# A one-core hybrid encoder block: dot products of the last 16 tokens before or after the start of the second expert pass

## The reference

```
idx = jnp.take_along_axis(cidx.reshape(TB, PH, K * K), pos, axis=-1)
g = jax.nn.softmax(top_s, axis=-1).astype(xb.dtype)
u = expert_u[idx]
a = jax.nn.gelu(jnp.einsum('td,thkd->thk', xb, u), approximate=False)
return jnp.einsum('thk,thkd->td', g * a, expert_v[idx])
```

## Time and profile before

| | us |
|---|---|
| three runs | 950.32, 951.26, 952.13 |
| median | 951.26 |
| the profiled execution's own time | 951.26 |
| its span, first to last instruction | 949.5 |

### The profile page before, as it was taken

The page is one execution under the profiler, slowest core; times in us unless marked ns, Lnnn a source line. Parts: engine busy times, 40 slices in busy tenths (PEclk is TensorE's granted clock), DMA queues, the critical chain, the costliest instruction groups (busy, mean ns, idle before and its releaser), DMA issues.

```text
span 949.5 us, 21518 instructions
## 1 busy us (share of the span) xinstructions
PE 942.1 (99%) x7332; PEld 905.1 (95%) x7332; DVE 780.5 (82%) x1622; ACT 557.4 (59%) x994; POOL 347.4 (37%) x202
## 2 busy tenths in 40 slices
PE   9999999999999999999999999999999999999997
PEld 9999899999999999999999999999999999999997
DVE  7988878889799997777787774788888888888776
ACT  6556764666665646666766765555555555555545
POOL 0000000067878787888888876111000100000000
PEclk9999999999999999999999999999999999999999
DMA  8887667666579998999999999999999999998981
GB/s 304 262 242 206 198 202 237 211 206 203 181 223 261 244 237 224 261 268 274 231 268 265 239 229 248 313 366 321 319 317 332 332 332 322 317 322 273 294 259 45
DMA packets 134332, 246.63 MB, mean 260 GB/s; under 512 B 32032, under 2 KB 81056, under 8 KB 134000
## 3 DMA queue, kind: packets, MB, share of 16 engines
q1 hardware_dynamic: 110656, 227.73, 74.8%
q0 software_dynamic: 23168, 17.12, 9.9%
q10 hardware_dynamic: 432, 0.80, 0.2%
HBM read 219.21 MB, written 26.35 MB: 259 GB/s over the span
## 4 chain that ended last, share of the span: by engine, by line
PE 94%; DVE 3%; issue 1%; ACT 1%; DMA 1%; DVEq 0%; ACTq 0%
PE pOO L1462 45%; PE pOO L1741 8%; PE pTT L1758 6%; PE pOO L1758 6%; PE pMM L1758 6%; PE pSS L1758 6%; PE pMM L1759 3%; PE pOO L1759 3%; PE pTT L1759 3%; PE pSS L1759 3%; DVE wlos L918 1%; PE pSS L1527 1%; PE pSS L1683 1%; PE pSS L1716 1%; PE pTT L1716 1%
## 5 line engine op out<-in xcount | busy, mean ns | idle before, releaser
L653 ACT ACTIVATE whis<-raw 128x1024 fp32r<-128x1024 f32 x326 | 344.2, 1057 | 172.6 <-PE pSS L1759 140.6
L1462 PE MATMUL pOO<-xhi,whis 128*128 128x240 f32 (+1 forms) x1040 | 288.1, 277 | 0.0
L1462 PE MATMUL pOO<-xlo,whis 128*128 128x240 f32 (+1 forms) x1040 | 286.1, 275 | 0.0
L1462 PE MATMUL pOO<-xhi,wlos 128*128 128x240 f32 (+1 forms) x1040 | 286.1, 275 | 0.0
L628 POOL DMA_INDIRECT g_scratch<-small x128 | 234.1, 1829 | 51.0 <-issue 37.0
L918 DVE TENSOR_TENSOR wlos<-raw,whis 128x1024 fp32r<-128x1024 f32 x172 | 209.1, 1219 | 42.7 <-ACT whis L653 42.1
L1462 PEld LDWEIGHTS pOO<-xhi,whis 128*128 128x128 f32 x1040 | 196.3, 189 | 1.4 <-issue 1.3
L1462 PEld LDWEIGHTS pOO<-xlo,whis 128*128 128x128 f32 x1040 | 196.3, 189 | 0.0
L1462 PEld LDWEIGHTS pOO<-xhi,wlos 128*128 128x128 f32 x1040 | 196.3, 189 | 0.0
L1343 DVE TENSOR_TENSOR wlos<-raw,whis 128x1024 fp32r<-128x1024 f32 x125 | 153.0, 1224 | 49.6 <-ACT whis L653 48.0
L596 POOL TENSOR_TENSOR wlos<-raw,whis 128x1024 fp32r<-128x1024 f32 x30 | 72.2, 2416 | 213.6 <-ACT whis L653 213.3
(11 more groups left out here) (297 smaller groups left out, 1976.5 us busy)
## 6 DMA issues: line engine op xcount, KB each, us to landing
raw<-in_stream SPq DMA_DIRECT2D x199, 512.0 KB, 4.4
raw<-in_vrows SPq DMA_DIRECT2D x128, 512.0 KB, 4.9
a_scratch<-ast SPq DMA_DIRECT2D x128, 120.0 KB, 3.1
held<-a_scratch SPq DMA_DIRECT2D x128, 120.0 KB, 4.5
g_scratch<-ghot SPq DMA_DIRECT2D x32, 256.0 KB, 4.5
held<-g_scratch SPq DMA_DIRECT2D x124, 64.0 KB, 4.3
biasm<-in_bias SPq DMA_DIRECT2D x8, 256.0 KB, 5.4
g_scratch<-small POOLq DMA_INDIRECT x128
```

The lines of the kernel that those rows point to most:

```text
L653: act.activation(whi[s], raw[s][:], ACT.Copy).then_inc(hi_ready, 1)
L1462: last = pe.matmul(dst, st, mv, start=(c == 0 and q == 0), stop=(c == len(terms) - 1 and q == 2))
```

## The change

The number of dot rounds in the U pass rises from 8 to 14. Their gathers go in threes ahead of scatter heads 3 to 6, and two ahead of head 7, which had none. Two dot rounds are left in the V pass, at other places. The first row of `expert_v` is gathered at V tile 2 in place of 31, the last at 99 in place of 91; rows are added behind groups 5 to 27 in place of 10 to 25. Apart from this the first two `low` products of the V pass move, on DVE, from ahead of the `wlos` of V tile 1 to behind it.

```diff
-DOTS_U = 8
-DOT_TILES_U = (65, 73, 76, 84, 89, 97, 105, 113)
-GATHERS_U = {3: (0, 1), 4: (2, 3), 5: (4, 5), 6: (6, 7)}
+DOTS_U = 14
+DOT_TILES_U = (65, 68, 73, 76, 81, 84, 89, 92, 97, 105, 108, 113, 119, 124)
+GATHERS_U = {3: (0, 1, 2), 4: (3, 4, 5), 5: (6, 7, 8), 6: (9, 10, 11), 7: (12, 13)}
...
-DOT_TILES = (2, 5, 8, 11, 15, 19, 23, 27)
-DOT_GROUPS = (2, 3, 4, 5, 6, 7, 8, 9)
-GELU_GROUPS = (2, 12)
-SHARE_GROUPS = (3, 13)
-ROW_TILES = tuple(31 + 4 * m for m in range(TOPK))
-ROW_GROUPS = tuple(10 + m for m in range(TOPK))
+DOT_TILES = (10, 20)
+DOT_GROUPS = (4, 7)
+GELU_GROUPS = (2, 9)
+SHARE_GROUPS = (3, 11)
+ROW_TILES = (2, 9, 16, 23, 33, 39, 45, 51, 57, 63, 69, 75, 81, 87, 93, 99)
+ROW_GROUPS = (5, 6, 8, 9, 10, 12, 13, 15, 16, 18, 19, 21, 22, 24, 25, 27)
...
-                if i == NE_TILES - 1:
-                    low(0, 0)
-                    low(1, 1)
                 low_w(T_U + i + LO_LEAD)
...
+            low(0, 0)
+            low(1, 1)
             low_w(T_V + LEAD - 1)
```

## The result

The changed kernel takes 958.75 us in the median of seven runs (953.05 to 960.94), against 951.26 for the kernel before. The ratio is 1.006, with a 95% interval of 1.0033 to 1.0089. So it is slower by 0.6%, where I had forecast no change and a time of 951.2 within 949.9 to 953.0. With the runs that belong to the profiles, eleven executions are known: 950.86, 953.05, 955.4, 957.6, 957.98, 958.41, 958.58, 958.75, 958.8, 958.91, 960.94. The profiled one is that of 957.98, with a span of 956.2. This scatter of 10 us is itself a finding, since the kernel before stayed within 4.5 us in 77 executions beside the experiments (949.47 to 953.99).

The account below looks back on a forecast made before the run. PE was taken to bound both passes. The seam gave -0.03 us and dots, gathers and rows of V cost 0, so 951.26 - 0.03 = 951.2 us, within 949.9 to 953.0.

Parts of the forecast that it names:

- The spare time: Table load before V tile 0: second piece lands 6.0 us before its reading, so POOL's delay costs PE 0.
- The delay: Six more gathers on POOL delay the scatters by 2.9 us, taken as one step, 2.7; far ends 5.4 and 7.9.
- the two gathers of head 7: On POOL ahead of head 7: they cost nothing, within a wait of 3.21 us; 1.4 at the high gather price.
- A dot doesn't hold POOL: U pass, DVE beside POOL: only a wlos holds a scatter back, read from the scatter of 457.73.
- Rival (3): Scatters end too late, six dots each holding one for 1.2 us: 3.3 us on PE, 954.5; chance 0.04.
- the two old stops: PE stops at V tiles 2 and 4 in the kernel before, 0.66 us together, forecast to swallow the seam's new stop.
- The seam: Between U and V pass: V tile 0 runs 0.63 us late, stops at tiles 2 and 4 vanish, net -0.03.
- The dots in the U pass: On DVE: six more dots at about 1.30 us each, 7.8 us moved from the V pass, cost 0.
- Rival (2): U pass: three gathers in a row crowd out tile loads, PE stops, 2 to 4 us, 954; chance 0.08.
- The rows of V: End of V pass: last add done at 898.1, PE takes the sum at 918.20, 20 us left, cost 0.

Follow-up runs that it names:

- experiment 5: The kernel before, unchanged, profiled a second time: 951.32 us.
- experiment 1: The kernel before with only the two low products of the seam moved behind the wlos of V tile 1: 951.09 us, ratio 1.0.
- experiment 4: The kernel before with six more DVE operations of a dot's kind and size in the U pass, results unused: 950.89 us, ratio 0.9995.
- experiment 12: The kernel before with the whis of V tile 2 ahead of the gelu of the last U tile: 951.96 us, ratio 1.0006.
- experiment 3: The kernel before with six more gathers at the changed kernel's places, into free buffers nobody reads: 956.58 us, ratio 1.0052.
- experiment 7: The changed kernel with 52 PE products on old data ahead of V tile 0: 957.35 us, ratio 1.0068.
- experiment 8: The kernel before with ten dots in the U pass, the two further gathers ahead of head 7: 951.22 us, ratio 1.0001.
- experiment 9: The changed kernel without the last four scatters of head 7: 950.9 us, ratio 0.9998.
- experiment 6: The kernel before with 5.03 us of memsets on POOL ahead of head 7, no DMA added: 955.95 us, ratio 1.0044.
- experiment 10: The changed kernel with one wlos less on POOL ahead of its first scatter, given to DVE: 952.89 us, ratio 1.0042.
- experiment 11: The kernel before with twelve dots in the U pass, third gathers at heads 3 to 6, none at head 7: 951.24 us, ratio 1.0013.
- experiment 2: The changed kernel with the two low products put back ahead of the wlos of V tile 1: 956.81 us, ratio 1.0039.

## Why the prediction was wrong

**The spare time (the step that failed first).** The prediction took 6.0 us between the landing of the table's second piece (load at 589.26, landed about 594.3) and its reading at 600.28. The arithmetic was right and the row was real, but it came from the earliest of five executions with that many gathers. In the others the load comes at 595.95 to 597.02, and the same sum (5.0 to land) leaves -0.7 to -1.7 us. In experiment 5 `weights` waits 1.94 us already; in 1, 4 and 12 it doesn't wait, as a piece can land in 2.4 us. A first sign stood in the groups: the earlier trace rows gives waits of 0.30 and 0.57 at heads 6 and 5 against 1.57 and 3.21 at heads 3 and 7, so the chain's length hung on how each wait fell. I used one execution for a margin that the next could lose.

**The delay (under-sized).** Forecast 2.9 us, taken as one step of a tile, 2.7, with 5.4 and 7.9 as ends. Against the usual chain of before it is one step in experiments 3 and 7 and two, 5.4 us, in the changed kernel; against the first profile it is five, 13.4. Seen against the second profile of before it is 4.4 at the table load and 5.2 at the last scatter; against the first one 12.1 and 12.9. The sum had gathers and waits, and put at nothing that the scatters themselves get slower; of the five steps they are 7.7 us. A gather was set at 1.26 with its issue. Those of the changed kernel take 1.34 + 0.30 in the mean, and at head 4 the second and third took 1.98 and 1.86. Heads 3 to 6 took 559.08 - 404.91 = 154.17 us to the next head's start, against 554.92 - 403.76 = 151.16 in the second profile of before. The forecast of nothing for the two gathers of head 7 was right in experiment 8, where 0.79 us of the wait were left; in the changed kernel they leave none. A later head 7 has more of its scatters in the last tiles, at 2.67 us each: ten, against eight in the second profile of before (571.65 to 590.32) and five in the first.

**"A dot doesn't hold POOL" (misread).** The row it was read from, the scatter of 457.73, had begun 0.72 us ahead of its dot. Where the dot begins first it holds the scatter to 1.42 us behind its own end, as a `wlos` does (495.20, experiment 4). The Trainium skill (SBUF — State Buffer, section on the two separate sides) says that a VectorE operation with two SBUF inputs and a GpSimd operation that reads SBUF exclude each other: whichever starts first has the port pair that they share for its whole length. The trace agrees for a dot or `wlos` that starts first. The other way round it doesn't show the rule, as a dot that starts behind a scatter takes its usual 1.22 to 1.27 us.

**The price of the stop (left out).** Rival (3) took PE's wait as the whole cost. With the wait comes a restart at half clock, 2.3 us after a stop of 5.6. The profiled execution lies 3.5 us over the rival's 954.5: a wait of 5.6 in place of 3.3 and the half clock, less the two old stops and a front shorter by 0.5.

**Rival (3) itself** named the right place, the scatters that end too late, with a chance of 0.04. Its mechanism, every one of six dots holding a scatter for 1.2 us, is not what happened: six more dots alone leave the chain at 305.63 us against 305.62, with a ratio of 0.9995 (experiment 4). Six more gathers alone make the loss (experiment 3). A held scatter can add to it: those of 495.20 and 498.07 are where the changed kernel falls behind experiment 7. The chance should have been built on the end of the scatters, by whatever cause, and not on that one cause.

**Right were** these steps. The seam: forecast 0.63 late at V tile 0 and no stop at tiles 2 and 4, seen so in experiment 9. The dots in the U pass at no cost on DVE, with PE at 155.00 of 155.00 us. Rival (2), crowding, doesn't happen: PE doesn't stop in the U pass. The rows of V in time: the last add is at 903.55, done at 904.83, and PE takes the sum at 924.91, 20 us later, as forecast. Beyond the restart at its start no time came from the V pass.

**Open.** That a few hundredths or tenths of a us decide whether a scatter or DVE's instruction goes first, and that the chain then differs by whole tiles, is in the rows. What moves those starts from one execution to the next isn't settled. Head 1 took 34.96 us in the first profile of before and 34.51 in experiment 6, in all other profiles 37.0 or more. Experiments 6, 10 and 11 show two groups of times, and I have profiles of the lower group only. Why a piece of the table lands in 2.5 us in one execution and in 5.4 in another isn't known either.

## What to carry to other kernels

A margin that ends a chain of a hundred small waits is a spread, not a number: before a change leans on it, look at a second profile, or at the same margin in any other profile of nearly the same kernel. Gathers hide in a queue's wait only as long as that wait lasts; the one that doesn't fit costs its full issue time, and everything behind it in the queue shares the bill. Where the end of such a chain meets a saturated PE, price the step, which is the wait and the restart at half clock together.

## What the runs showed of the hardware

- PE's clock and the stop before it: after stops of 0.40 to 1.22 us (experiments 1, 5, 9, 12) nothing changed; after 3.19 us (experiment 3) the clock fell about 0.7 us after the restart and was 0.50 for some 3.4 us; in stops of 4.44 and 5.59 us (experiment 2, the changed kernel) it had fallen before PE went on, and was 0.50 from the first product on, for about 6 and 4.4 us. With products on old data through the wait it stayed at 1.00. From V tile 0 to the products of the sum it took 317.03, 318.23 and 317.49 us in these three, and 315.20 at full clock: 1.8 to 3.0 us.
- POOL's scatters and DVE: the one that begins first goes on, and a scatter that begins under a running `wlos` or dot (1.22 us each) ends 1.4 us or more behind it. The same scatter took 1.55 us when it began 0.01 us ahead of a `wlos` and 2.52 when it began 0.12 behind (experiment 5).
- Two executions with the same span of 949.5 us differed by 7.75 us in when POOL loaded the table behind its last of 128 scatters. A time doesn't tell where an engine off the critical path stands.
- In the changed kernel indirect gathers of 128 rows took POOL 0.94 to 1.98 us to issue for the same shape, and scatters 1.54 to 3.74.
